# Expert down projection on one core: the first pair of every eight tiles (32 to 119) as seven block products

## What is computed

```python
def expert_block(args):
    xb, eb, gb = args
    ub = jnp.take(u, eb, axis=0)
    act = jax.nn.gelu(jnp.einsum('thkd,td->thk', ub, xb), approximate=False)
    vb = jnp.take(v, eb, axis=0)
    return jnp.einsum('thk,thkd->td', gb * act, vb)
...
x = layer_norm(DN_ALPHA * x + peer_ffn(x, ...), ln_g[i, 1], ln_b[i, 1])
```

## Time and profile before

| | us |
|---|---|
| median of three runs | 2619.03 (2618.84 to 2619.05) |
| the profiled execution, device time | 2619.5 |
| its span, first to last instruction | 2617.7 |
| TensorE busy, share of the span | 2579.7, 99% |
| VectorE, ScalarE, GpSimd busy | 1738.9, 1498.3, 669.4 |
| mean granted TensorE clock | 0.998 |

### The profile page before, as it was taken

The page is one execution under the profiler, slowest core; times in us unless marked ns, Lnnn a source line. Parts: engine busy times, 40 slices in busy tenths (PEclk is TensorE's granted clock), DMA queues, the critical chain, the costliest instruction groups (busy, mean ns, idle before and its releaser), DMA issues.

```text
span 2617.7 us, 43833 instructions
## 1 busy us (share of the span) xinstructions
PE 2579.7 (99%) x14973; PEld 2212.8 (85%) x14978; DVE 1738.9 (66%) x3203; ACT 1498.3 (57%) x2863; POOL 669.4 (26%) x310
## 2 busy tenths in 40 slices
PE   8999999999999999999999999999999999999998
PEld 7789998887888887799988887888888887877887
DVE  4568778886555565459778885555567746555774
ACT  4445588885455554454588884445556545564553
POOL 0007876772000000018877771000001000001000
PEclk9999999999999999999999999999999999999999
DMA  6255544445565554355544456666556665535564
GB/s 224 81 165 176 182 161 154 155 159 197 193 192 192 192 169 146 105 163 183 178 158 156 154 164 201 193 193 192 192 177 196 187 196 168 161 109 162 168 192 153
DMA packets 124331, 447.66 MB, mean 171 GB/s; under 512 B 14312, under 2 KB 14952, under 8 KB 123936
## 3 DMA queue, kind: packets, MB, share of 16 engines
q1 hardware_dynamic: 120096, 434.16, 51.8%
q0 software_dynamic: 2608, 9.08, 1.2%
q10 hardware_dynamic: 1488, 2.59, 0.3%
HBM read 444.74 MB, written 1.05 MB: 170 GB/s over the span
## 4 chain that ended last, share of the span: by engine, by line
PE 93%; DVE 2%; ACT 2%; DMA 1%; issue 1%; POOL 0%; ACTq 0%; DVEq 0%; POOLq 0%
PE ps L827 42%; PE ps L783 20%; PE ps L788 10%; PE ps L799 4%; PE ps L805 4%; PE ps L802 4%; PE ps L1046 3%; PE ps L1118 1%; PE ps L1015 1%; ACT w_hi L434 1%; PE ps L887 1%; PE ps L734 0%; PE ps L1064 0%; DMA ring<-in_v 0%; DMA ring<-in_ffn_in 0%
## 5 line engine op out<-in xcount | busy, mean ns | idle before, releaser
L434 ACT CAST w_hi<-ring 128x1024 fp32r<-128x1024 f32 (+1 forms) x812 | 852.1, 1050 | 761.7 <-PE ps L827 513.5
L446 DVE TENSOR_TENSOR w_lo<-ring,w_hi 128x1024 fp32r<-128x1024 f32 x545 | 664.7, 1220 | 553.6 <-ACT w_hi L434 544.4
L446 POOL TENSOR_TENSOR w_lo<-ring,w_hi 128x1024 fp32r<-128x1024 f32 x267 | 640.5, 2399 | 838.5 <-ACT w_hi L434 639.9
L827 PE MATMUL ps<-w_hi,x_parts 128*128 128x512 f32 x2976 | 745.4, 391 | 4.1 <-ACT w_hi L434 2.5
L827 PEld LDWEIGHTS ps<-w_hi,x_parts 128*128 128x128 f32 x2976 | 554.2, 188 | 125.7 <-issue 8.2
L783 PE MATMUL ps<-x_parts,w_hi 128*128 128x512 f32 x2320 | 592.0, 397 | 0.7 <-ACT w_hi L434 0.6
L783 PEld LDWEIGHTS ps<-x_parts,w_hi 128*128 128x128 f32 x2320 | 416.0, 189 | 76.3 <-ACT w_hi L434 1.1
L827 PE MATMUL ps<-w_lo,x_parts 128*128 128x512 f32 x1488 | 402.6, 389 | 0.4 <-DVE w_lo L446 0.3
L788 PEld LDWEIGHTS ps<-x_parts,w_lo 128*128 128x128 f32 x2320 | 316.5, 190 | 22.6
L827 PEld LDWEIGHTS ps<-w_lo,x_parts 128*128 128x128 f32 x1488 | 278.2, 188 | 59.5 <-DVE w_lo L446 1.7
L788 PE MATMUL ps<-x_parts,w_lo 128*128 128x256 f32 x2320 | 323.0, 282 | 0.0
(11 more groups left out here) (287 smaller groups left out, 2280.0 us busy)
## 6 DMA issues: line engine op xcount, KB each, us to landing
ring<-in_u SPq DMA_DIRECT2D x256, 512.0 KB, 3.5
ring<-in_v SPq DMA_DIRECT2D x256, 512.0 KB, 4.3
ring<-in_ffn_in SPq DMA_DIRECT2D x88, 512.0 KB, 4.0
ring<-in_ffn_out SPq DMA_DIRECT2D x44, 512.0 KB, 4.2
ring<-in_wq SPq DMA_DIRECT2D x32, 512.0 KB, 3.5
ring<-in_ple_gate SPq DMA_DIRECT2D x16, 512.0 KB, 4.3
SC<-in_rows POOLq DMA_DIRECT2D x11, 512.0 KB, 5.0
ring<-in_a_qk SPq DMA_DIRECT2D x8, 512.0 KB, 4.5
```

The costliest lines, as they stand in the source:

```text
L434: nc.scalar.copy(part(w_hi, i)[:, used(name)], tile(i)[:, used(name)]).then_inc(tiles_hi, 1)
L446: eng.tensor_tensor(part(w_lo, i)[:, at], tile(i)[:, at], part(w_hi, i)[:, at], ALU.subtract).then_inc(tiles_low[LOW[n][0]], 1)
L827: mm = nc.tensor.matmul(acc[:, 2 * tb + f, 0:cnt], x[:, k + c, tb * P:(tb + 1) * P], part(w, i)[:, at:at + cnt], start=(first and n == 0 a ...
```

## The change

In tiles 32 to 119 of each layer, eleven bodies of eight tiles, the first two tiles of each body are done together. Their product is 2 blocks of tokens x 2 tiles times 2 tiles x 2 halves of columns, and it is computed with seven block products (Strassen's scheme in Winograd's form) in place of eight. With three terms each that is 21 matmuls of 128x512 in place of 24. The other six tiles of a body stay as they were.

- TensorE (`mixed_pair`): two products with parts of the first tile (6 matmuls), three with sums of weight blocks (9), two with parts of the second tile (6). Some products go to `acc`, four stay apart in PSUM banks 4 to 7 over the whole stage.
- VectorE makes, one body ahead, three sums of activation blocks (`rows_mixed`) and four sums of weight blocks (`block_sum`), and their low parts (`rows_low`, `sums_lower`). ScalarE makes the high parts (`rows_high`, `sums_high`).
- In these bodies activations are staged two tiles at a time (`stage_pair`, 128x512), at steps 0, 2, 5 and 7 of a body: for the tiles 2, 4, 6 and 8 after its first.
- SyncE loads the two tiles of a pair into two buffers of their own, in `big` where the activations of tiles 0 to 31 lay. The order of loads in a body changes (`stream_mixed`).
- The four banks are added into X during tiles 121 to 125 (`fold`, seven VectorE instructions), and `layer_norm` there takes the weight 1.0 for DN_ALPHA. The side projection is copied out at tiles 24 to 27.

```diff
+MIX_FROM, MIX_TO = 32, 120
+MIX_AT = (0,)
...
+                def mixed_pair(m, b, turns=0, first=False, last=False):
+                    name, p = f"v{layer}", pairs_before(layer, b, m)
+                    j = MIX_FROM + BODY * b + MIX_AT[m]
+                    i, k = TILE[name] + j, j % BODY
+                    hi_here(name, j, turns)
+                    pe.wait_ge(staged, turns * BODY + (EXPERT_TILES * layer + j + 2))
+                    pe.wait_ge(mixed_low, turns * MIX_PAIRS + (p + 1))
...
+                    mm = products([(c11, raw(k, one), halves_of(i, left)), (c12, row(3), halves_of(i, right))],
+                                  lambda: lo_here(name, j, turns), lambda dst: False)
+                    begins_tile(mm)
+                    pe.wait_ge(sums_low, turns * (2 * MIX_PAIRS) + 2 * (p + 1))
+                    mm = products([(c21, raw(k, two), sums(2)), (own[1], row(0), sums(0)), (own[2], row(2), sums(1))],
+                                  None, lambda dst: dst is not c21)
+                    begins_tile(mm)
+                    hi_here(name, j + 1, turns)
+                    mm = products([(own[0], raw(k + 1, one), halves_of(i + 1, left)),
+                                   (own[3], row(1), halves_of(i + 1, right))],
+                                  lambda: lo_here(name, j + 1, turns), lambda dst: True)
...
ScalarE:
+                def stage_pair(j, turns=0):
+                    act.wait_ge(tiles_begun, turns * BODY + (TILE[f"v{layer}"] + j + 1 - BODY + 2))
+                    S.copy(x_hi[:, j % BODY:j % BODY + 2, :].rearrange("p a b -> p (a b)"), pair_rows(j, turns)
+                           ).then_inc(staged_hi, 2)
...
+                    for j in range(BODY):
+                        if j == 0:
+                            act.wait_ge(pair_sums, turns * 4 + 4 * (pairs_before(layer, b, 0) + 1))
+                        take_high(act, name, at + j + 1, turns)
+                        for ahead in {0: (2,), 2: (4,), 5: (6,), 7: (8,)}.get(j, ()):
+                            stage_pair(at + ahead, turns)
+                        if last:
+                            continue
+                        if j == 3:
+                            rows_high(b + 1, turns)
+                        elif j == 6:
+                            sums_high(b + 1, slice(0, 2), turns)
+                        elif j == 7:
+                            sums_high(b + 1, slice(2, 3), turns)
...
VectorE:
+                    for j in range(BODY):
+                        take_low(dve, name, at + j + 1, turns)
+                        for ahead in {0: (2,), 2: (4,), 5: (6,), 7: (8,)}.get(j, ()):
+                            stage_pair(at + ahead, turns)
+                        if last:
+                            continue
+                        if j == 1:
+                            rows_mixed(b + 1, turns)
+                        elif j == 3:
+                            block_sum(0, b + 1, turns)
+                            rows_low(b + 1, turns)
+                        elif j == 4:
+                            block_sum(1, b + 1, turns)
+                            block_sum(2, b + 1, turns)
+                        elif j == 5:
+                            block_sum(3, b + 1, turns)
+                        elif j == 6:
+                            sums_lower(b + 1, slice(0, 2), turns)
+                        elif j == 7:
+                            sums_lower(b + 1, slice(2, 3), turns)
...
before body 0, tiles 24 to 31:
+                for j in range(MIX_FROM - BODY, MIX_FROM):
+                    n = j - (MIX_FROM - BODY)
+                    take_low(dve, f"v{layer}", j + 1)
+                    stage(j + 2)
...
+                rows_low(0)
+                sums_lower(0, slice(2, 3))
...
-                layer_norm(f"v{layer}", f"ln{layer}_1")
+                folded(FOLDS)
+                layer_norm(f"v{layer}", f"ln{layer}_1", 1.0)
```

More of the change, by code:

```diff
@@ L201, with in_mix, in_pair_buffer, landing_counts @@
                  "ffn2_in")
+def in_mix(name, j):
+    return name in ("v0", "v1") and MIX_FROM <= j < MIX_TO
+def in_pair_buffer(name, j):
+    return in_mix(name, j) and j % BODY in (OWN_PAIR, OWN_PAIR + 1)
+def landing_counts():
+    out, done = [], {}
+    for name, n in STREAM:
+        for j in range(n):
+            where = (in_pair_buffer(name, j), (j if in_pair_buffer(name, j) else len(out)) % RING)
+            done[where] = done.get(where, 0) + 1
+            alone = in_mix(name, j) and (in_pair_buffer(name, j) or (j - OWN_PAIR) % BODY in (RING, RING + 1))
+            out.append((where, done[where], 1 if alone else BODY // RING))
+    return out
+LANDED = landing_counts()
 def low_on_pool(name, j):
@@ L1074, in down, with raw, row, halves_of @@
                     split_wide(f"v{layer}", j, (x_hi, x_lo), j % BODY, j == 0, j == EXPERT_TILES - 1, turns)
+                def mixed_pair(m, b, turns=0, first=False, last=False):
[5 more added lines that the diff above has]
+                    pe.wait_ge(mixed_low, turns * MIX_PAIRS + (p + 1))
+                    one, two = slice(0, P), slice(P, T)
+                    left, right = slice(0, 512), slice(512, D)
+                    def raw(kk, tokens):
+                        return x_hi[:, kk, tokens], x_lo[:, kk, tokens]
+                    def row(n):
+                        return row_hi[:, n], row_lo[:, n]
+                    def halves_of(ii, at):
+                        return part(w_hi, ii)[:, at], part(w_lo, ii)[:, at]
+                    def sums(n):
+                        return sum_hi[:, n], sum_lo[:, n]
+                    def products(group, low, apart):
+                        begun = None
+                        for n in range(3):
+                            if n == 2 and low:
+                                low()
+                            for dst, x, w in group:
+                                mm = nc.tensor.matmul(dst, x[n % 2], w[n // 2], start=(first and apart(dst) and n == 0),
+                                                      stop=(last and apart(dst) and n == 2))
+                                begun = begun or mm
+                        return begun
+                    own = [ps[:, 4 + n, :] for n in range(4)]
+                    c11, c12, c21 = (acc[:, n, :] for n in range(3))
+                    mm = products([(c11, raw(k, one), halves_of(i, left)), (c12, row(3), halves_of(i, right))],
[9 more added lines that the diff above has]
+                                  lambda: lo_here(name, j + 1, turns), lambda dst: True)
+                    mm.then_inc(sums_used, 1)
@@ L1076, in peer, with mixed_body @@
+                def mixed_body(b, turns=0, first=False, last=False):
+                    for s in (0, 4):
+                        if s in MIX_AT:
+                            mixed_pair(MIX_AT.index(s), b, turns, first, last and s == MIX_AT[-1])
+                        for j in range(s + 2 if s in MIX_AT else s, s + 4):
+                            down(MIX_FROM + BODY * b + j, turns)
+                        first = first and MIX_AT[0] > s
                 for j in range(BODY):
                     down(j)
-                with pe.Fori(1, EXPERT_TILES // BODY - 1, 1) as turns:
+                with pe.Fori(1, MIX_FROM // BODY, 1) as turns:
@@ L1079, in peer @@
                     for j in range(BODY, 2 * BODY):
                         down(j, turns - 1)
-                for j in range(EXPERT_TILES - BODY, EXPERT_TILES):
+                moved(pe, SLOT[f"ple_proj{layer}"], 4)
+                mixed_body(0, first=True)
+                with pe.Fori(1, MIX_BODIES - 1, 1) as turns:
+                    mixed_body(1, turns - 1)
+                mixed_body(MIX_BODIES - 1, last=True)
+                for j in range(MIX_TO, EXPERT_TILES):
                     down(j)
+                pe.wait_ge(mix_folded, FOLDS * (layer + 1))
@@ new lines, in rows_low, with block_sum @@
+                def rows_low(b, turns=0):
+                    p = pairs_before(layer, b, 0)
+                    dve.wait_ge(mixed_hi, turns + (p + 1))
+                    V.tensor_tensor(row_lo[:], row_sums[:], row_hi[:], ALU.subtract).then_inc(mixed_low, 1)
+                def block_sum(n, b, turns=0):
+                    p, i = pairs_before(layer, b, 0), TILE[f"v{layer}"] + MIX_FROM + BODY * b
+                    b21, b22 = tile(i)[:, 0:512], tile(i)[:, 512:D]
+                    b11, b12 = tile(i + 1)[:, 0:512], tile(i + 1)[:, 512:D]
+                    if n == 0:
+                        tile_here(dve, i, turns)
+                        tile_here(dve, i + 1, turns)
+                        if b:
+                            dve.wait_ge(sums_low, turns * 2 + 2 * p)
+                    else:
+                        dve.wait_ge(pair_sums, turns * 4 + (4 * p + n))
+                    out, one, two = ((block_sums[:, 0], b11, b12), (block_sums[:, 1], block_sums[:, 0], b22),
```

(12 more changed lines are left out.)

229 lines of the change are left out of this document (206 added, 23 removed).

## The result

| | before | changed |
|---|---|---|
| median of the runs, us | 2619.04 (4 runs) | 2644.82 (2643.43 to 2645.66, 4 runs) |
| ratio to before | | 1.0098, 95% interval 1.0086 to 1.0109 |
| span of the profiled execution, us | 2617.7 | 2640.9 |

What follows compares the result with a forecast made beforehand. TensorE, busy 99% of the span, was taken as the bound. Against 2619.5 us: - 15.0 for matmuls, + 38.7 for two waits per body, + 2.4 ahead of body 0, less 0.5 for the median: 2645 us, range 2626 to 2660.

Steps and rivals of the forecast that it cites:

- The removed matmuls: Pairs on TensorE: 21 matmuls in place of 24, 66 fewer at 0.2267 us each, saving 15.0 us.
- The two waits: TensorE waits for staged activations before tile 6 and the next pair, 0.88 us each, + 38.7 us over 22 bodies.
- Ahead of body 0: Before the first mixed body the pair waits for `rows_low`: 1.2 us in each layer, 2.4 us in all.
- VectorE in time: VectorE ends step 4 at 13.86 us, before the next `w_lo` can start at 14.01; 0.15 us spare, nothing counted.
- rival 3: VectorE late in step 4, delaying tile 6 by 0.3 to 0.8 us per body: 2652 to 2663 us; chance 0.20.
- the first: Rival: waits before tiles 6 and 8 don't bite, the matmul count decides: 2604 to 2606 us; chance 0.08.
- the second: Rival: only one of the two waiting places in a body bites: 2626 us; chance 0.07.
- The transfers: Loads of a pair's two tiles, 4.3 us to land, fit by 1.3 us before VectorE wants them.
- The folds: Seven folds at the stage's end, some 5.8 us of VectorE, counted as zero; 1 us a layer if they don't fit.

Runs made afterwards that it cites:

- the first experiment: Changed kernel with the activation staging of steps 5 and 7 put ahead of the weights' cast and low part: 2607.39 us, ratio 0.9957 to the kernel before.
- the experiment with one place: Changed kernel with the activation staging put ahead of the weights' cast and low part at step 5 only: 2626.55 us, ratio 1.0035 to the kernel before.

## Why the prediction was right

**The removed matmuls** were worth their time, 66 x 0.2267 = 15.0 us. The bodies of the first experiment are 21.08 us (one in each layer is 0.07 longer), 0.68 below 21.76; times 22 that is 15.0. The assumption that a matmul of the pair costs the same as any other holds: a wrong one would have moved this sum.

**The two waits.** Each link, predicted from the cast's start and then read: staging starts at 2.23 and 2.23 (814.37 - 812.14), takes 0.68 and 0.68, next cast 0.64 after its end and 0.67 (815.72 - 815.05), the tile after the restart 0.05 longer and 0.03. I put 0.88 on each. By the means of all 22 bodies a body has 22.84 - 21.09 = 1.75 us of waiting, 0.87 for each wait. 44 of them: 38.5 where I had 38.7.

**Ahead of body 0**: 3.90 - 2.72 = 1.18 us in each layer where I had 1.2, and the wait named `row_lo`, as the step said.

**VectorE in time.** It had 0.17 us to spare at the one tight place, where I had 0.15: the two block sums of step 4 take 1.41 us together, where 0.68 + 0.07 + 0.68 is 1.43. Here I was near an edge: some 0.5 us more in step 4 (an estimate: the 0.17 to spare and the 0.3 at which rival 3 begins) would have made rival 3 true. The two 128x128 sums, for which there was no row, took 0.29 each (I took 0.3); they stand in step 1, where VectorE had 0.7 us to spare. The third rival, whose upper end of 2663 lay outside the range to 2660, which was said to take it in, fell by those 0.17 us, the first by the timeline, the second by the experiment with one place.

**The transfers** fitted: no wait on a pair's landing, and a load of a pair landed after 3.9 us (median) where I took 4.3. **The folds** at the end did too: the casts of tiles 121 to 127 are 2.72 to 2.74 apart, and no matmul there waited for a low part.

**The whole.** The first instruction of the layer norm behind the stage, line by line before and after (its first and last start are those of two of the four norms):

```profile
L1950 DVE SCALAR_TENSOR_TENSOR X<-X,ps x4: 1220/1220/1221, 142.6 to 1934.0; 128x1024 f32<-128x1024 f32 x4
...
L1064 PEld LDWEIGHTS ps<-ring,SC x32: 187/190/192, 613.6 to 1584.9; 128*128 128x128 f32 x32
```

```profile
L2207 DVE SCALAR_TENSOR_TENSOR X<-X,ps x4: 1220/1222/1222, 139.9 to 1958.0; 128x1024 f32<-128x1024 f32 x4
...
L1198 PEld LDWEIGHTS ps<-ring,SC x32: 187/190/192, 611.0 to 1596.3; 128*128 128x128 f32 x32
```

From the side projection's last weight load to the norm, layer 1 took 1934.0 - 1584.9 = 349.1 us before and 1958.0 - 1596.3 = 361.7 after: 12.6 more. In layer 0 the same two instructions start at 619.76 and 968.49 before, at 617.10 and 979.31 after: 13.5 more. Together 26.1, the sum of the prediction; the three terms as measured above come to 25.9. The profiled execution's span grew by only 23.2, mostly because it was already 142.6 - 139.9 = 2.7 us ahead at the first norm, in a stage that the change doesn't touch: its 2643.43 us is the lowest of the four runs. The median, 25.8 above that of before, is the better measure. That the sum fits to within half a microsecond is luck in part; the runs of these kernels spread by 2 to 8 us.

## What to carry to other kernels

- Where an engine off the bottleneck looks too full by its sum of busy time, look at the order first: for each operand that the bounding engine asks for first, follow the chain that makes it back to the last event that it may not pass, here the buffer that comes free when the tile before begins. Whatever the chain is longer than one tile is paid in full each time, and neither a lighter load nor a faster instruction beside the chain gives anything back.
- Put what is asked for first ahead of what is asked for late. Two edits of order, with the same instructions, turned 1.0% slower into 0.5% faster.
- The distance from start to start of one instruction that occurs once per tile shows a stall to 0.01 us, where the time of a run is uncertain by 2 us.

## What the runs showed of the hardware beyond that

- What a dependency within VectorE costs is not one number. The next instruction starts 0.08 to 0.09 us before the end of the one before when it needn't wait for it (814.37 against 813.23 + 1.23). The second of the two 128x512 sums of step 4 waits for the count of the first, and the two take 1.41 us at 0.685 each: it starts 0.04 after the end. Of the 128x128 sums the second reads the first, and they start 0.44 us apart at 0.29 us each: 0.15 after the end. I had taken 0.07 for the pair of 128x512. Why the 128x128 wait longer stays open. The lines of the changed kernel, first the pair of 128x512:

```profile
811.65 1.41 DVE L2581 TENSOR_TENSOR big<-big 128x512 f32<-128x512 f32 x2
...
826.45 0.29 DVE L2557 TENSOR_TENSOR big<-big 128x128 f32<-128x128 f32 x1
826.89 0.29 DVE L2559 TENSOR_TENSOR big<-big 128x128 f32<-128x128 f32 x1
```

- The kernel with VectorE relieved by 17 us in 200 had TensorE's time unchanged to 0.01 us (190.00 in both), so no contention between the two for memory shows in these two runs.
